# Wide router products, residual sums in halves, and the second memory head's softmax steps moved ahead, in a float32 two-block kernel

## What is computed

```python
# cross attention over the memory, 4 heads of 128
sc = jnp.einsum('bshd,bmhd->bhsm', q, kv[:, :, 0]) * CA_HEAD_DIM ** -0.5
p = jax.nn.softmax(sc, axis=-1)
x = x + o @ wo
# experts: each takes the 32 tokens that like it best
logits = jnp.einsum('bnd,de->bne', rmsnorm_2(x, g), router_w)   # 256 x 16
aff = jax.nn.softmax(logits, axis=-1)
gates, idx = lax.top_k(jnp.swapaxes(aff, 1, 2), 32)
xs = h[idx]                                  # 16 experts x 32 tokens x 1024
ys = (silu(xs @ w_gate) * (xs @ w_up)) @ w_down * gates
x = rmsnorm_2(x + scatter_add(idx, ys), final_norm_g)
```

## Time and profile before

| | |
|---|---|
| median of three runs | 1523.83 us |
| the profiled execution | 1523.98 us |
| its span (first to last instruction) | 1522.2 us |
| PE busy | 1229.4 us, 81% |
| DVE busy | 385.7 us, 25% |
| ACT busy | 292.3 us, 19% |
| DMA, mean over the span | 329 GB/s |
| the same, slices 18 to 39 of 40 | 426 to 429 GB/s |

### The profile page before, as it was taken

The page is one execution under the profiler, slowest core; times in us unless marked ns, Lnnn a source line. Parts: engine busy times, 40 slices in busy tenths (PEclk is TensorE's granted clock), DMA queues, the critical chain, the costliest instruction groups (busy, mean ns, idle before and its releaser), DMA issues.

```text
span 1522.2 us, 17032 instructions
## 1 busy us (share of the span) xinstructions
PE 1229.4 (81%) x7375; PEld 734.5 (48%) x7375; DVE 385.7 (25%) x587; ACT 292.3 (19%) x409; POOL 30.7 (2%) x32
## 2 busy tenths in 40 slices
PE   8999999999999999986666766757757757767666
PEld 7899789999878566431321321312313313313211
DVE  5755464555366754100000000000000000000001
ACT  5543544333364543000000000000000000000001
POOL 1000000000030100000000000000000000000000
PEclk9999999999999998888878778688787787688788
DMA  9754436555544376999999999999999999999997
GB/s 339 256 176 160 162 111 208 181 168 206 191 155 112 111 309 257 364 427 426 427 427 429 428 427 427 428 427 428 428 427 428 428 428 428 427 428 428 426 428 294
DMA packets 84470, 500.95 MB, mean 329 GB/s; under 512 B 4878, under 2 KB 29652, under 8 KB 59588
## 3 DMA queue, kind: packets, MB, share of 16 engines
q1 hardware_dynamic: 83204, 495.59, 80.8%
q0 software_dynamic: 1216, 4.63, 0.9%
HBM read 499.15 MB, written 1.05 MB: 329 GB/s over the span
## 4 chain that ended last, share of the span: by engine, by line
PE 51%; DMA 45%; ACT 2%; DVE 1%; issue 1%; SPq 0%; POOLq 0%; POOL 0%; DVEq 0%; ACTq 0%
DMA arena<-in_expert_w_gu_dram 35%; PE psA L620 12%; PE psA L609 11%; DMA arena<-in_expert_w_down_dram 10%; PE psB L1202 5%; PE psB L1166 4%; PE psB L801 4%; PE psB L1133 3%; PE psA L961 2%; PE psA L812 1%; PE psA L1013 1%; PE psB L1057 1%; PE psB L652 1%; DVE x_res L2188 1%; PE psA L780 0%
## 5 line engine op out<-in xcount | busy, mean ns | idle before, releaser
L1166 PE MATMUL psB<-arena,x_res 128*32 128x512 f32 x2048 | 327.5, 774 | 212.6 <-DMA arena<-in_expert_w_gu_dram 212.6
L1166 PEld LDWEIGHTS psB<-arena,x_res 128*32 128x32 f32 x2048 | 63.7, 126 | 451.1 <-DMA arena<-in_expert_w_gu_dram 328.7
L1672 DVE TENSOR_TENSOR split_r<-arena,split_r 128x2048 fp32r<-128x2048 f32 x75 | 171.6, 2291 | 178.2 <-ACT split_r L1250 178.2
L1250 ACT CAST split_r<-arena 128x2048 fp32r<-128x2048 f32 x77 | 146.4, 1906 | 206.5 <-PE psA L620 109.6
L620 PE MATMUL psA<-hT_r,split_r 128*128 128x256 f32 x1536 | 185.2, 283 | 0.0
L620 PEld LDWEIGHTS psA<-hT_r,split_r 128*128 128x128 f32 x1536 | 184.7, 192 | 0.2
L1575 ACT ACTIVATE x_res<-psB 128x512 f32<-128x512 f32 x16 | 9.6, 597 | 849.3 <-PE psB L1166 849.3
L609 PE MATMUL psA<-split_r,hT_r 128*128 128x512 f32 x720 | 167.1, 391 | 1.4 <-issue 0.8
L1202 PE MATMUL psB<-arena 128*32 128x512 f32 x1024 | 143.3, 715 | 6.6 <-DMA arena<-in_expert_w_down_dram 6.0
L609 PEld LDWEIGHTS psA<-split_r,hT_r 128*128 128x128 f32 x720 | 134.0, 188 | 30.2 <-issue 2.6
L1133 PE MATMUL psB<-sb_b,arena 128*128 (+1 forms) x512 | 107.6, 390 | 11.4 <-ACT arena L1577 11.2
(11 more groups left out here) (345 smaller groups left out, 797.0 us busy)
## 6 DMA issues: line engine op xcount, KB each, us to landing
arena<-in_expert_w_gu_dram SPq DMA_DIRECT2D x128, 2048.0 KB, 35.4
arena<-in_expert_w_down_dram SPq DMA_DIRECT2D x63, 2048.0 KB, 36.4
arena<-in_w_in_dram SPq DMA_DIRECT2D x36, 1024.0 KB, 7.6
arena<-in_w_gate_dram SPq DMA_DIRECT2D x11, 1024.0 KB, 5.4
arena<-in_w_up_dram SPq DMA_DIRECT2D x11, 1024.0 KB, 8.0
arena<-in_w_down_dram SPq DMA_DIRECT2D x10, 1024.0 KB, 6.1
arena<-in_w_out_dram SPq DMA_DIRECT2D x6, 1024.0 KB, 5.5
arena<-in_ca_wkv_dram SPq DMA_DIRECT2D x4, 1024.0 KB, 6.3
```

The lines of the kernel that those rows point to most:

```text
L1166: ins = pe.matmul(psB[32 * j:32 * j + 32, o, :], XC[:, k, :], w[:, o * EFF + j * NC:o * EFF + (j + 1) * NC], start=(k == 0), stop=(k == GU ...
L1250: a.copy(W_HI[n % 2].rearrange("p (k n) -> p k n", k=view.shape[1]), view).then_inc(sig("hi_ready"), 1)
L1672: v.tensor_tensor(W_LO[n % 2].rearrange("p (k n) -> p k n", **shape), view, W_HI[n % 2].bitcast(F32).rearrange("p (k n) -> p k n", **shape ...
```

## The change

The second head's maximum goes ahead of the weight splitting on DVE, and its exponentials ahead of the fourth query copy on ACT:

```diff
             ca_max(0)
             ca_norm(0)
+            ca_max(1)
             split_lo("wo", 0)
-            ca_max(1)
             ca_norm(1)
...
             ca_queries(2)
+            ca_exp(1)
             ca_queries(3)
-            ca_exp(1)
```

```diff
+            pe.wait_ge(sig("x4_ready"), 3)
+            turn_last(1, range(0, KT // 2))
+            residual_sum(0, 0, 0)
+            pe.wait_ge(sig("x4_ready"), 4)
+            turn_last(1, range(KT // 2, KT))
+            residual_sum(0, 0, 1)
             pe.wait_ge(sig("wr_ready"), 1)
-            router(0)
-            turn_tile("n5", psA, 1, "x4_ready")
-            ins = router(1)
+            for k in range(KT):
+                wait_h("n5", k, 1)
+                j = k % 4
+                ins = pe.matmul(psB[32 * j:32 * j + 32, 0, 0:TOK], WR[:, k, :], HT5[:, k, :],
+                                start=(k < 4), stop=(k >= 4), skip_group_check=True)
             ins.then_inc(sig("router_mm"), 1)
-            for t in range(TT):
-                residual_sum(1, t)
+            residual_sum(1, 0, 0)
+            pe.wait_ge(sig("lg_ready"), 1)
+            for t in range(TT):
+                ins = pe.matmul(psB[:, 2, t * NE:(t + 1) * NE], LGP[:, t * P:(t + 1) * P], C("fold", NE), start=True, stop=True)
+            ins.then_inc(sig("router_mm"), 1)
+            residual_sum(1, 0, 1)
+            for half in range(2):
+                residual_sum(0, 1, half)
             pe.wait_ge(sig("aff_ready"), 1)
...
-            for t in range(TT):
-                ins = residual_sum(0, t)
+            for half in range(2):
+                ins = residual_sum(1, 1, half)
             ins.then_inc(sig("sums"), 1)
-            keep_warm(psB[:, 3, :], 2)
+            keep_warm(psB[:, 3, :], 3)
```

The transposes of tile 0 now wait for both of its quarters (`x4_ready` 2) and go to other PSUM banks; each copy of them takes 128 x 256 elements in place of two of 128 x 128. ACT squares the last quarter of x after all its copies. On DVE the copy of the partial sums stands ahead of the root:

```diff
             stream_square("x4_ready", 0, SQ5)
+            tile_copies("n5", 0, HT5)
             stream_square("x4_ready", 1, SQ5)
-            tile_copies("n5", 0, HT5)
+            tile_copies("n5", 1, HT5)
             stream_square("x4_ready", 2, SQ5)
-            tile_copies("n5", 1, HT5)
...
+            dve.wait_ge(sig("router_mm"), 1)
+            v.tensor_copy(LGP, psB[:, 0, 0:TOK]).then_inc(sig("lg_ready"), 1)
             residual_root("n5")
-            dve.wait_ge(sig("router_mm"), 1)
+            dve.wait_ge(sig("router_mm"), 2)
```

At the first expert the second gather call moves behind slot 0, and one product of 256 columns that only keeps PE at work takes its place:

```diff
             gather(0, 3, range(0, 2))
-            gather(0, 2, range(2, 4))
+            keep_warm(psB[:, 2, 0:TOK], 1)
...
                         w = expert_slot(k)
+                        if first and k == 1:
+                            gather(0, 2, range(2, 4))
                         if first and k == 2:
                             gather(0, 3, range(4, KT))
```

More of the change, by code:

```diff
@@ L72 @@
 CONSTS = [("ident", P), ("anti", P), ("le", P), ("ones", P), ("le_rev", P), ("ones2", P),
-          ("iota", CAP), ("cos", TT * 32), ("sin", TT * 32)]
+          ("iota", CAP), ("fold", NE), ("cos", TT * 32), ("sin", TT * 32)]
 CCOL = {}
@@ L108, in constants @@
     put("iota", np.tile(np.arange(1, CAP + 1), (P, 1)))
+    put("fold", (np.arange(P)[:, None] % 32 == np.arange(NE)[None, :]) * 1.0)
     t = np.arange(TOK)
@@ L143, in build @@
         cols = sb("cols", NROW)
-        wr2 = sb("wr2", KT * NE)
+        wr2 = sb("wr2", KT * 32)
         pw = sb("pw", 4 * 64, parts=64)
@@ L271, in build @@
         TKW = vs_b[0:NE, 1280:1536]
+        LGP = vs_b[:, 0:TOK]
+        WR = wr2[:, :].rearrange("p (k n) -> p k n", k=KT)
         SS, VV, RR, T_a, T_b = st[:, 0:4], st[:, 4:24], st[:, 24:44], st[:, 44:64], st[:, 64:84]
@@ L446, in copy_no, with turned_last @@
             return b // 2 + 1 + TILE_TURNS.index(tag) * 4 + 2 * t
+        def turned_last(t, b):
+            if t == 0:
+                return psB[:, 2 * (b % 2), (b // 2) * TOK:(b // 2 + 1) * TOK]
+            return (psA[:, 1, 0:TOK], psA[:, 3, 0:TOK], psB[:, 1, 0:TOK], psB[:, 3, 0:TOK])[b]
         def lo_signal(n):
@@ L660, in turn_tile @@
                     pe.wait_ge(sig(x_ready), 2 * t + k // (KT // 2) + 1)
-                    if t == 1 and tag in TILE_TURNS:
-                        wait_h(tag, k, 0)
                     ins = pe.transpose(ps[:, k // 2, (k % 2) * TOK + t * P:(k % 2) * TOK + (t + 1) * P],
                                        X[:, t, k * P:(k + 1) * P], ident)
-                    if k % 2 == 1 and (t == 1 or tag in TILE_TURNS):
+                    if k % 2 == 1 and t == 1:
                         ins.then_inc(sig("turned"), 1)
@@ L1005, in _, with turn_last, residual_sum @@
                         turn_tile("n4", psB, c, "x3_ready")
+            def turn_last(t, ks):
+                for k in ks:
+                    ins = pe.transpose(turned_last(t, k // 2)[:, (k % 2) * P:(k % 2 + 1) * P], X[:, t, k * P:(k + 1) * P], ident)
+                    if k % 2 == 1:
+                        ins.then_inc(sig("turned"), 1)
+            def residual_sum(c, t, half):
+                sl = slice(half * TOK, (half + 1) * TOK)
+                return pe.matmul(psA[:, 2 * c + t, sl], ident, X[:, t, c * NC + sl.start:c * NC + sl.stop], start=(half == 0), stop=(half == 1),
+                                 skip_group_check=True)
             def queries(f):
@@ L1061, in ca_out @@
                         if h == CA_H - 1 and t == 1 and c == 0:
-                            turn_tile("n5", psA, 0, "x4_ready")
+                            pe.wait_ge(sig("x4_ready"), 2)
+                            turn_last(0, range(KT))
                 if h % 2 == 1:
@@ L1220, in _, with tile_copies @@
             a = nc.scalar
-            def tile_copies(tag, t, dst, row=None):
+            def tile_copies(tag, t, dst):
                 for b in range(0, 4, 2):
[L1225 to L1230, removed]
+                    act.wait_ge(sig("turned"), turn_no(tag, max(b, 2 - 2 * t), t))
+                    a.copy(dst[:, 2 * b:2 * b + 2, t * P:(t + 1) * P],
+                           turned_last(t, b).rearrange("p (k n) -> p k n", k=2)).then_inc(sig("hT_act"), 1)
             SQ5 = [XN[:, 0, :], XN[:, 1, 0:NC], XN[:, 1, NC:D]]
@@ L1558, in _ @@
             stream_square("x4_ready", 0, SQ5)
+            tile_copies("n5", 0, HT5)
             stream_square("x4_ready", 1, SQ5)
-            tile_copies("n5", 0, HT5)
+            tile_copies("n5", 1, HT5)
             stream_square("x4_ready", 2, SQ5)
-            tile_copies("n5", 1, HT5)
-            act.wait_ge(sig("lg_ready"), 1)
+            act.wait_ge(sig("lg_ready"), 2)
             for t in range(TT):
-                ins = a.activation(AFF[:, t, :], psB[:, 0, t * NE:(t + 1) * NE], ACT.Exp, bias=T_a[:, t:t + 1], scale=RR[:, t:t + 1],
+                ins = a.activation(AFF[:, t, :], psB[:, 2, t * NE:(t + 1) * NE], ACT.Exp, bias=T_a[:, t:t + 1], scale=RR[:, t:t + 1],
                                    accum_out=T_b[:, t:t + 1])
@@ L1601, in _ @@
             nc.gpsimd.memset(power[:, :], -0.5).then_inc(sig("power_set"), 1)
-            pool.wait_ge(sig("power_set"), 1)
+            nc.gpsimd.memset(wr2[:, :], 0.0).then_inc(sig("power_set"), 1)
+            pool.wait_ge(sig("power_set"), 2)
             root("n1")
@@ L1611, in _ @@
             pool.dma_start(wg2.rearrange("p (k n) -> p k n", k=KT), k_major(w_in2)[:, :, W2["gates"]:W2["gates"] + 16]).then_inc(sig("small_loaded"), 16)
-            pool.dma_start(wr2[:, :].rearrange("p (k n) -> p k n", k=KT), k_major(A["router_w_2"][0])).then_inc(sig("small_loaded"), 16)
+            pool.dma_start(WR[:, :, 0:NE], k_major(A["router_w_2"][0])).then_inc(sig("small_loaded"), 16)
             pool.dma_start(pw[:, :].rearrange("p (g n) -> p g n", g=4), A["pool_w_2"][0].rearrange("g c n -> c g n")).then_inc(sig("small_loaded"), 16)
@@ L1853, in _ @@
             operand_lo("n3", ROW["norm_mix_g_2"])
-            w = wr2[:, :].rearrange("p (k n) -> p k n", k=KT)
+            w = WR[:, :, 0:NE]
             g = cols[:, ROW["norm_ffn_g_2"]:ROW["norm_ffn_g_2"] + KT]
@@ L2063, in tile_copies @@
                 for b in range(1, 4, 2):
[L2064 to L2067, removed]
+                    dve.wait_ge(sig("turned"), turn_no(tag, max(b, 3 - 2 * t), t))
+                    v.tensor_copy(dst[:, 2 * b:2 * b + 2, t * P:(t + 1) * P],
+                                  turned_last(t, b).rearrange("p (k n) -> p k n", k=2)).then_inc(sig("hT_dve"), 1)
             def residual_root(tag):
@@ L2122, in _ @@
                         tile_copies("n5", c, HT5)
+            dve.wait_ge(sig("router_mm"), 1)
+            v.tensor_copy(LGP, psB[:, 0, 0:TOK]).then_inc(sig("lg_ready"), 1)
             residual_root("n5")
[L2125 to L2126 removed]
+            dve.wait_ge(sig("router_mm"), 2)
+            link(v.tensor_reduce(T_a[:, 0:2], psB[:, 2, 0:2 * NE].rearrange("p (t e) -> p t e", t=TT), AX.X, ALU.max, negate=True))
             v.tensor_tensor(T_a[:, 0:2], T_a[:, 0:2], RR[:, 0:2], ALU.mult).then_inc(sig("lg_ready"), 1)
```

9 lines of the change are left out of this document (removed).

## The result

The changed kernel takes 1516.52 us (median of five runs, 1515.92 to 1518.54), the kernel before, timed beside it, 1525.42 us (1523.72 to 1525.56). The ratio is 0.995 with a 95% interval of 0.9938 to 0.9961, so it is 6 to 9.5 us faster. The forecast was 1516.4. The profiled execution took 1516.52 us; its span is 1514.7 us, 7.5 us less than before.

A forecast was written before the change was run, and what follows sets the result against it. The end was taken to follow load 11's issue, which starts the full expert-weight stream at 427 GB/s. Terms -1.2 - 3.4 - 2.8 = -7.4 us took the profiled 1523.98 to 1516.6, median 1516.4; range 1513.6 to 1521.0.

The forecast's parts named there:

- The issue of load 11: Start of the expert-weight stream: each microsecond this issue comes earlier is one off the time; 617.66 to 610.2.
- the condition that the prediction named: Start of the expert stream: load 11's issue counts as long as load 10 is done by 1.7 us after it.
- 6.8 us for load 10: Load 10, issued into an empty queue, is done 6.8 us after its issue, 1.9 us later than its transfer needs.
- Part 1: Cross attention: second head's maximum and exponentials first remove ACT's idle time; -1.2 us, ends 0 and -1.4.
- Part 2: Router up to selection: maximum 1.7 us earlier, first MAX8 3.4 us earlier in all.
- Rival B: Router: column groups don't overlap, or the root comes later; 1.8 us less gain, time 1518.3; chance 0.08.
- Part 3: Gather to slot 2: 7.9 us at full clock in place of 10.65; -2.8 us, all of it the clock.
- the split buys an earlier load 10 but load 11 waits: Split gather: load 10 issued at about 604.9 before the shift, but load 11 waits for slot 2 behind the same work.
- Rival A: Thin stretch behind keep_warm: clock falls once more, slots 0 and 1 lose 2.8 us; time 1519.6; chance 0.20.
- The sum: Up to load 11: -1.2 - 3.4 - 2.8 = -7.4 us, load 11 at 610.2, median 1516.4.
- The rule on transposes: Router: transposes don't count as TensorE activity as products do, making a clock fall there more likely.
- rival C: Clock falls already in the router, picks come at about 602.5; time 1521.5; chance 0.08.

The follow-up runs named there:

- e1: Kernel before with only the second head's maximum and exponentials moved ahead; ratio to before 0.9986 (0.9977 to 0.9995).
- e7: Changed kernel with the third gather call behind slot 2 in place of before it; median 1516.61 us.
- e8: Changed kernel with the third gather call behind slot 2 and DVE's mean issued to POOL ahead of its wait for the router products; median 1516.09 us.
- e13: Kernel e8 plus two 512-column products that keep PE at work in the first block's attention at 188 us; 1515.07 us, ratio to before 0.9942.
- e3: Kernel before with only the second gather call moved behind slot 0 and one 256-column product in its place; ratio to before 1.0004 (0.9995 to 1.0014).
- e10: Changed kernel with both first gathers again ahead of slot 0 and no 256-column product; median 2.2 us over the changed kernel.
- e11: Changed kernel without the one 256-column product behind the first gather call, split gather kept; median 2.1 us over the changed kernel.
- e9: Changed kernel with the earlier second-head maximum and exponentials undone; median 4.6 us over the changed kernel.
- e12: Changed kernel with two keep_warm products of 512 columns in place of three behind the sums; median 1.2 us over the changed kernel.
- e5: Changed kernel without any product that only keeps PE at work between the affinities and slot 0; median 4.9 us over the changed kernel.
- e2: Kernel before with only the wide router, half sums, third keep_warm product and router orders of ACT and DVE; ratio to before 0.9978 (0.9966 to 0.9989).

## Why the prediction was right

Step by step:

- *What decides.* "The issue of load 11" held: over the thirteen profiles taken after before's, whose load 11 lies between 607.3 and 617.8, the rest is 904.2 to 906.1 us. It is not the issue of load 10: e1 has it at 611.01 and before at 611.15, but e1's load 11 comes 1.2 us earlier and its end 1.6. Where load 11 comes under 5 us after load 10 (e7, e8, e13), load 10 seems to take over, the condition that the prediction named. Its 6.8 us for load 10 were too few: the trace has the landing 7.5 us after the issue before and 7.7 after. In the changed kernel that is 611.0, still ahead of load 11's issue plus 1.7, 611.6.
- *Part 1*, -1.2 forecast, -1.37 measured. PE kept 0.47 us of idle time before `ca_turn(2)`, so the wait there shrank by 0.89 us; the rest was gained before it, 0.41 us of it at `ca_turn(1)`, which the sum didn't have.
- *Part 2*, -1.7 and -1.7 forecast, -1.82 and -1.83 measured. The second half is the clock and PE's order together: M8 follows the maximum by 3.96 us where the sums ran at half clock (before, e1, e3), by 2.13 in all others. The three also have the old order, so no run separates the two. Rival B's price was mis-sized: 2.5, not 1.8.
- *Part 3*, -2.8 forecast, -2.54 measured; "the split buys an earlier load 10 but load 11 waits" held (load 10 to load 11 6.61 us, before 6.51), and that it is all the clock: with the clock up from the gather on, part 3 alone also had 8.11 (e3), and by e10 the old order at full clock would take about 7.4. The forecast had 7.9: a slot takes 1.86 us from its start to the next gather, not 1.75.
- *Rival A*, a further fall in front of slot 0, is real. In the order of the changed kernel it costs 1.5 to 5.0 us (G to S2 9.62 in e11, 9.75 in e9, 11.16 in e12, 13.07 in e5, against 8.11) where the forecast had 2.8 and a little. It did not happen in the changed kernel's profiled execution but did in those of e2, e5, e9, e10, e11 and e12; e9 even has all of parts 2 and 3. With both products one profile in six shows a fall (e9), near the chance of 0.20 that it was given: that the changed kernel's profiled execution had none is in part luck. Whether the changed kernel's two slower runs (1517.55, 1518.54) had it, or the long dense part, isn't shown.
- What I did not see is the 1.5 us of the dense part. It falls on either kernel. The profiled executions of before and changed both have the short one, which is why a sum made against one execution came out. Three of before's five runs beside the changed kernel lie at 1525.4 to 1525.6 and would fit the long one, but none of the five has a profile; the profiled execution, 1523.98, is another.
- *The sum* closes: start 0.2, part 1 1.4, part 2 3.65, part 3 2.5 make load 11's 7.8 us, and 0.3 us more behind it leave 7.5. The terms missed by 0.2 to 0.3 us each, in both directions. That the forecast is within 0.1 us of the median is luck: the medians measured side by side differ by 8.9 us, not by the 7.4 of the sum, which went from 1523.83.
- Two figures of the prediction are slightly off and change nothing: 180 loads stand behind load 11, not 181 (192 in all, counted from 0), and its terms put load 11 at 611.5 before the shift, not at 611.3.

The rule on transposes from the Trainium skill ("TensorE: Matmul & The Clock Gate", PE-mode transpose), which spoke for rival C, had no occasion to show: with the transposes set between sums and wide products the clock held through the router in every profile of the new form.

## What to carry to other kernels

When a queue of transfers is the bound, look for the one issue at which it fills for good, date the rest from there, and price every edit by that date; work before it that doesn't move it is free. An engine's clock is part of its critical path: fill idle time in thin stretches with wide products on a bank that nobody reads, but only where an interval of the trace shows that they end before what they bridge. Where single executions differ by more than the effect, compare intervals between fixed events of the traces before medians.

## What the runs showed of the hardware

- The dense part has two lengths, 1.5 us apart on average (start at 556.7 to 557.7, or 558.4 to 559.3). All long ones in fourteen profiles (e1, e2, e3, e5, e8, e9) have the clock at a half from about 190 to 194 us, none of the others has. From the first transpose at 190 to the 512-column products behind it is 5.2 us in each of the six and 3.5 in each of the eight. PE idles 2.07 us just before, in all but e13, and then does only transposes and 128-column products; so the idle time alone doesn't tell when the clock falls.
- A fall in front of slot 0 lasted 3.4 us at the least (e1, e9, e10, e11) and 13.6 at the most (e5).
- Load 10, issued into an empty queue, landed 7.5 us after its issue before and 7.7 us in the changed kernel, in place of the 4.9 us that its bytes take in the stream; with the next load issued 4.6 us after it the queue no longer ran empty (371 and then 377 GB/s in e7's rows).
- The four column groups gave 3.4 times the rate of one (3.64 to 1.07 us for eight products of 256 columns).
